# One core, a mixer and a three-pass MLP: VectorE's extra steps set one at a time at 13 spots of a group, and the first weight block of the second mixer half reloaded in parts

## What is computed

```python
def _rmsnorm(x, g): return x * rsqrt(mean(x * x) + EPS) * g
# mixer: u = hn @ w_in (1024 x 3072); an RG-LRU group and an HGRN2 group; y @ w_out
xp = xp + mixer(_rmsnorm(xp, ln_mix))
pn = _rmsnorm(xp, ln_mlp)
xp = xp + jnp.square(jax.nn.relu(pn @ w_up)) @ w_down       # D_FF = 4096
y = _rmsnorm(xp, ln_final)
```

## Time and profile before

| what | value |
|---|---|
| three runs | 2414.80, 2419.99, 2423.82 us |
| profiled execution | 2409.82 us, its span 2408.0 us |
| mean granted clock of TensorE | 0.974 |
| TensorE matmuls busy | 2253.4 us, 94% |
| VectorE busy | 1576.2 us, 65% |
| ScalarE busy | 1114.3 us, 46% |
| GpSimd busy | 1028.8 us, 43% |

### The profile page before, as it was taken

One profiled execution on the slowest core, in us unless ns is written; L12 is line 12 of the kernel. 1 busy time (PEld: TensorE's weight loads), 2 busy tenths in 40 slices (PEclk: granted clock), 3 DMA queues, 4 the chain that ended last, 5 costly groups with the idle time before them and its releaser, 6 DMA issues.

```text
span 2408.0 us, 43738 instructions
## 1 busy us (share of the span) xinstructions
PE 2253.4 (94%) x16512; PEld 2132.1 (89%) x16512; DVE 1576.2 (65%) x2884; ACT 1114.3 (46%) x2281; POOL 1028.8 (43%) x884
## 2 busy tenths in 40 slices
PE   9999999789999997999999978998889997899997
PEld 7878889778899987999999978998889997899997
DVE  8766663866666568766765286777676665765557
ACT  5444542445555554344344144554445454445554
POOL 2142102257777761000000035665556754566663
PEclk9999999899999998999999989999999999999998
DMA  9999955467765463322225334445556943354443
GB/s 347 274 300 293 260 159 209 129 182 207 205 175 168 144 188 94 105 88 89 83 76 189 110 108 158 136 135 168 159 168 181 315 119 95 107 158 151 133 129 115
DMA packets 239024, 397.78 MB, mean 165 GB/s; under 512 B 30944, under 2 KB 147808, under 8 KB 238816
## 3 DMA queue, kind: packets, MB, share of 16 engines
q1 hardware_dynamic: 187248, 262.71, 34.4%
q0 software_dynamic: 35872, 103.66, 16.6%
q10 hardware_dynamic: 15696, 28.61, 3.4%
HBM read 334.22 MB, written 127.77 MB: 192 GB/s over the span
## 4 chain that ended last, share of the span: by engine, by line
PE 72%; DVE 12%; ACT 6%; DMA 4%; issue 4%; POOL 2%; ACTq 1%; SPq 0%; DVEq 0%; POOLq 0%
PE bank L1068 10%; PE bank L1070 9%; PE bank L1069 9%; PE bank L1325 7%; PE bank L1327 6%; PE bank L1326 6%; PE aux L1325 6%; PE aux L1327 6%; PE aux L1326 6%; ACT w_hi L1416 2%; DVE dense L2593 2%; DMA w_st<-up_sums 2%; ACT dense L1416 2%; POOL w_lo L941 1%; PE aux L1265 1%
## 5 line engine op out<-in xcount | busy, mean ns | idle before, releaser
L941 POOL TENSOR_TENSOR w_lo<-w_st,w_hi 128x512 fp32r<-128x512 f32 x672 | 882.4, 1339 | 597.5 <-ACT w_hi L1416 596.3
L1416 ACT ACTIVATE w_hi<-w_st 128x512 fp32r<-128x512 f32 (+1 forms) x704 | 450.8, 649 | 518.9 <-PE aux L1327 273.7
L1068 PE MATMUL bank<-a_hi,w_hi 128*128 128x360 f32 (+4 forms) x1344 | 480.3, 357 | 14.6 <-DMA w_lo<-kept_lo 11.9
L1070 PE MATMUL bank<-a_hi,w_lo 128*128 128x360 f32 (+4 forms) x1344 | 462.8, 344 | 0.0
L1069 PE MATMUL bank<-a_lo,w_hi 128*128 128x360 f32 (+4 forms) x1344 | 462.3, 344 | 0.0
L1325 PE MATMUL bank<-dense,w_hi 128*128 128x328 f32 (+2 forms) x768 | 256.3, 334 | 36.1 <-DVE dense L2593 22.1
L1325 PE MATMUL aux<-dense,w_hi 128*128 128x328 f32 (+2 forms) x768 | 252.6, 329 | 37.5 <-DVE xy L2660 37.5
L1068 PEld LDWEIGHTS bank<-a_hi,w_hi 128*128 128x128 f32 x1344 | 253.9, 189 | 37.5 <-DVE xy L2660 8.1
L1069 PEld LDWEIGHTS bank<-a_lo,w_hi 128*128 128x128 f32 x1344 | 254.5, 189 | 16.8 <-issue 1.6
L1070 PEld LDWEIGHTS bank<-a_hi,w_lo 128*128 128x128 f32 x1344 | 253.9, 189 | 16.2
L1327 PE MATMUL aux<-dense,w_lo 128*128 128x328 f32 (+2 forms) x768 | 250.3, 326 | 0.0
(11 more groups left out here) (322 smaller groups left out, 4395.8 us busy)
## 6 DMA issues: line engine op xcount, KB each, us to landing
w_st<-up_sums SPq DMA_DIRECT2D x192, 256.0 KB, 2.7
w_st<-down_sums SPq DMA_DIRECT2D x384, 128.0 KB, 2.2
w_st<-in_wall SPq DMA_DIRECT2D x144, 256.0 KB, 2.7
w_st<-in_wall SPq DMA_DIRECT2D x288, 128.0 KB, 2.3
up_sums<-in_wall POOLq DMA_DIRECT2D x40, 512.0 KB, 13.8
down_sums<-in_wall POOLq DMA_DIRECT2D x40, 512.0 KB, 20.8
w_st<-in_wall SPq DMA_DIRECT2D x32, 512.0 KB, 8.0
kept_hi<-w_hi SPq DMA_DIRECT2D x32, 512.0 KB, 9.8
```

The lines of the kernel that those rows point to most:

```text
L941: pool.tensor_tensor(w_place(w_lo, h), w_place(w_st, h), w_place(w_hi, h).bitcast(F32), ALU.subtract).then_inc(w_ready, 1)
L1068: pe.matmul(ps, wh, xh, start=(j == 0), stop=False)
L1070: mm = pe.matmul(ps, wl, xh, start=False, stop=(j == 7))
L1416: return nc.scalar.activation(out, in_, func, **kw)
```

## The change

VectorE's extra steps get 13 numbered spots in a group, one step at each: spots 0 to 2 ahead of the up stage's first gather, 3 and 4 behind the first and second gather, and in the down stage spot 5 + 2j inside pair j, between take 6 and takes 2, 3 and 4, and spot 6 + 2j behind the pair. spare(q, g, n) says what stands at a spot. ScalarE's high parts and squares and SyncE's stores are placed to suit (SPOT_AT, SPOT_STORE). The operands ahead begin at spot 8 of group 2 and end at spot 4 of group 6. The sums of squares stand in groups 1 and 2 of pass 2, TensorE's sum and ScalarE's root in group 3, the two inverses in groups 4 and 5, the scaling in groups 5 and 6, and the stores of it in groups 6 and 7. Of to_basis only the first pair's two additions stay between the quarters; the others go to spots 5 to 10.

At the handover the first weight block is reloaded in two column halves, each as soon as its old content is used up and before both of GpSimd's adds, with semaphores of its own; the second add goes behind the reload of block 1. The loads of x are issued up to two halves later, and NF, FN and FY three slots later. basis_pair and unmix are cut into halves of one instruction each (basis_half, unmix_half; the waits stay).

The parts of the diff are in the order of the file: constants, SyncE, GpSimd, TensorE, ScalarE, VectorE.

```diff
-LATE = 1
+LATE = 2
-X_LOADS = {15: (0, 1), 16: (2,), 18: (3,), 19: (4,), 21: (5,), 22: (6,), 23: (7,)}
+X_LOADS = {15: (0,), 17: (1,), 18: (2,), 20: (3,), 21: (4,), 22: (5,), 23: (6, 7)}
...
-AHEAD_G = 3
 RIGHT_D[2] = [s_ for steps in AHEAD for s_ in steps]
-STORE_AT = [23, 26, 30, 33]
+SPOT_AT = {3: 0, 4: 1, 5: 14, 6: 15, 7: 17, 8: 19, 9: 21, 10: 22, 11: 24, 12: 26}
+SPOT_STORE = {3: 9, 4: 10, 5: 23, 6: 25, 7: 27, 8: 28, 9: 30, 10: 32, 11: 34, 12: 35}
+SPOTS = 13
+
+def _ahead_spots():
+    at, g, n = {}, 2, 8
+    for op in RIGHT_D[2]:
+        while n < 3 and op[0][0] == "l":
+            n += 1
+        at[g, n] = op
+        g, n = (g, n + 1) if n + 1 < SPOTS else (g + 1, 0)
+    return at
+
+AHEAD_AT = _ahead_spots()
+HIGH_AT = {(g, SPOT_AT[n]): ("hi" + op[0][2], op[1]) for (g, n), op in AHEAD_AT.items() if op[0][0] == "l"}
+STORE_AT = {HALVES * g + SPOT_STORE[n]: RIGHT_A.index(("hi" + op[0][2], op[1]))
+            for (g, n), op in AHEAD_AT.items() if op[0][0] == "l"}
+ADD_AT = {(1, n): n - 3 for n in range(3, 13)} | {(2, n): n + 7 for n in range(3, 9)}
+SQUARE_AT = {(g, SPOT_AT[n]): m for (g, n), m in ADD_AT.items()}
...
-FINAL_SLOTS = {9: ("NF", 0), 10: ("FN", 0), 11: ("FN", 1), **{13 + b: ("FY", b) for b in range(8)}}
+FINAL_SLOTS = {12: ("NF", 0), 13: ("FN", 0), 14: ("FN", 1), **{16 + b: ("FY", b) for b in range(8)}}
...
-                for n in range(len(AHEAD)):
-                    if h - STREAM == HALVES * (AHEAD_G + n // PAIRS) + STORE_AT[n % PAIRS]:
-                        keep_ahead(2 * n)
-                        keep_ahead(2 * n + 1)
+                if h - STREAM in STORE_AT:
+                    keep_ahead(STORE_AT[h - STREAM])
...
+            pool.wait_ge(w_kept[0], 32 * (MLP0 // 2))
+            for half in range(2):
+                c = slice(HW * half, HW * (half + 1))
+                pool.wait_ge(product_done, down_no(0, GROUPS - 1, PAIRS - 1, ORDER[2 * half]))
+                pool.dma_start(w_hi[:, 0, c], kept_hi[0][:, c]).then_inc(w_first[half], 16)
+                pool.dma_start(w_lo[:, 0, c], kept_lo[0][:, c]).then_inc(w_first[half], 16)
             add_input_square(1 + DVE_SQUARES)
-            pool.wait_ge(w_kept[0], 32 * (MLP0 // 2))
-            pool.wait_ge(product_done, down_no(0, GROUPS - 1, PAIRS - 1, ORDER[2]))
-            reload(0, 0)
-            add_input_square(2 + DVE_SQUARES)
             pool.wait_ge(w_kept[1], 32 * (MLP0 // 2))
             pool.wait_ge(product_done, down_no(0, GROUPS - 1, PAIRS - 1, ORDER[-1]))
             reload(1, 1)
+            add_input_square(2 + DVE_SQUARES)
...
-                if p and blk < MLP0:
-                    pe.wait_ge(w_again[blk % 2], 32 * (blk // 2 + 1))
+                if p and blk == 0:
+                    pe.wait_ge(w_first[0], 32)
+                elif p and blk < MLP0:
+                    pe.wait_ge(w_again[blk % 2], 32 * ((blk + 1) // 2))
...
+                    elif p and (blk, t) == (0, 0):
+                        pe.wait_ge(w_first[1], 32)
...
+                    if q == 1 and (g, at) in HIGH_AT:
+                        act.wait_ge(next_normed, 2 * KB)
+                        right_high(2, *HIGH_AT[g, at])
+                    if q == 2 and (g, at) in SQUARE_AT:
+                        final_square(1, SQUARE_AT[g, at] // 4, SQUARE_AT[g, at] % 4)
...
-                        if q == 1 and AHEAD_G <= g < AHEAD_G + 4 and at in (17, 20, 24, 27):
-                            n = PAIRS * (g - AHEAD_G) + (17, 20, 24, 27).index(at)
-                            if n < len(AHEAD):
-                                for name, kb in RIGHT_A[2 * n:2 * n + 2]:
-                                    right_high(2, name, kb)
-                        elif (q, g) == (2, LATE) and at in (18, 22, 25):
-                            final_squares(1, (at - 18) // 3)
...
-                        if part == 2 and g in (LATE + 2, LATE + 3):
-                            t = g - LATE - 2
+                        if part == 2 and g in (6, 7):
+                            t = g - 6
...
-                    if i == 7 and g:
+                    if i == 7 and g == 0:
+                        dve.wait_ge(basis, 2 * (PAIRS * q + j + 1))
+                    elif i == 7:
                         dve.wait_ge(product_read, take_no(q, g - 1, j, 4))
...
+                    spare(q, g, 5 + 2 * j)
...
-                def to_basis(q):
-                    if q == 1:
-                        dve.wait_ge(old_in[2], 16 * KB)
-                    if q < 2:
-                        for j in range(PAIRS):
-                            basis_pair(q, j)
-                    dve.wait_ge(basis, PAIRS * (q + 1))
+                def spare(q, g, n):
+                    if q < 2 and g == 0 and 5 <= n < 11:
+                        basis_half(q, (n - 3) // 2, (n - 5) % 2)
+                    if q == 1 and g in (1, 2):
+                        if g == 1 and n >= 5:
+                            next_norm(n - 5)
+                        elif g == 2 and n < 8:
+                            next_norm(8 + n)
+                    if q == 1 and (g, n) in AHEAD_AT:
+                        dve.wait_ge(next_normed, 2 * KB)
+                        right_step(2, *AHEAD_AT[g, n])
+                    if (q, g) == (1, GROUPS - 1) and n >= 5:
+                        basis_half(2, (n - 5) // 2, (n - 5) % 2)
+                    if q == 2 and g == 0 and n >= 5:
+                        unmix_half(1, (n - 5) // 2, (n - 5) % 2)
+                    if q == 2 and (g, n) in ADD_AT:
+                        add_final(1, ADD_AT[g, n])
+                    if q == 2 and g in (LATE + 2, LATE + 3) and n == 0:
+                        middle_inverse(g - LATE - 2)
+                    if q == 2 and g in (5, 6) and n >= 5:
+                        middle_out(KB * (g - 5) + n - 5)
...
-                    to_basis(q)
+                    if q < 2:
+                        for half in range(2):
+                            basis_half(q, 0, half)
...
+                    for n in range(3):
+                        spare(q, g, n)
                     for j in range(2):
-                        for i in (5, 7, 6):
+                        for n, i in enumerate((5, 7, 6)):
                             gather(q, g, j, i)
+                            if j == 0 and n < 2:
+                                spare(q, g, 3 + n)
                         quarters(q, g, j)
...
                         takes(q, g, j)
+                        spare(q, g, 6 + 2 * j)
-                        elif q == 1 and g in (1, 2):
-                            for n in range(2):
-                                next_norm(KB * (g - 1) + 2 * j + n)
-                        elif q == 1 and AHEAD_G <= g < AHEAD_G + 4:
-                            n = PAIRS * (g - AHEAD_G) + j
-                            if n < len(AHEAD):
-                                for name, kb in AHEAD[n]:
-                                    right_step(2, name, kb)
-                        elif (q, g) == (1, GROUPS - 1):
-                            basis_pair(2, j)
-                        elif (q, g) == (2, 0):
-                            unmix(1, j)
-                        elif (q, g) == (2, LATE):
-                            for i in range(4):
-                                add_final(1, 4 * j + i)
-                        elif (q, g) == (2, LATE + 1):
-                            for i in range(4):
-                                middle_out(4 * j + i)
```

More of the change, by code:

```diff
@@ L517, in build @@
         w_again = [sem("w_again0"), sem("w_again1")]
+        w_first = [sem("w_first0"), sem("w_first1")]
         unit_done = sem("unit_done")
@@ L2392, in weight_rest, with unmix_half, unmix @@
                    ALU.subtract).then_inc(w_ready, 1)
-            def unmix(q, j):
+            def unmix_half(q, j, half):
                 x11, x12, x21, x22 = quadrants(q, j)
                 dve.wait_ge(product_read, take_no(q, GROUPS - 1, j, 4))
-                tt(x12, x12, x22, ALU.subtract).then_inc(unmixed, 1)
-                tt(x21, x21, x22, ALU.add).then_inc(unmixed, 1)
+                if half == 0:
+                    tt(x12, x12, x22, ALU.subtract).then_inc(unmixed, 1)
+                else:
+                    tt(x21, x21, x22, ALU.add).then_inc(unmixed, 1)
+            def unmix(q, j):
+                for half in range(2):
+                    unmix_half(q, j, half)
             for p in range(2):
@@ L2690, in takes, with basis_half @@
                         unmix(q, j)
-                def basis_pair(q, j):
+                def basis_half(q, j, half):
                     x11, x12, x21, x22 = quadrants(q, j)
-                    tt(x12, x12, x22, ALU.add)
-                    tt(x21, x21, x22, ALU.subtract).then_inc(basis, 1)
-                def to_basis(q):
-                    if q == 1:
-                        dve.wait_ge(old_in[2], 16 * KB)
-                    if q < 2:
-                        for j in range(PAIRS):
```

(15 more changed lines are left out.)

9 lines of the change are left out of this document (1 added, 8 removed).

## The result

The changed kernel takes 2345.25 us (median of 4 runs, 2340.55 to 2349.92) against 2417.39 before (4 runs, 2413.68 to 2423.82): ratio 0.970, 95% interval 0.967 to 0.973. Run once more beside other kernels it gave 2344.31 and 0.970 (0.967 to 0.972). The forecast was 2350, its range 2334 to 2390. The profiled execution took 2349.92, the longest of the four; its span is 2348.1.

A forecast was written before the change was run, and what follows sets the result against it. TensorE, 94% busy, plus its waits for VectorE's late takes was taken as the bound. Terms 29.1 + 2.6 + 25.3 + 7.3 + 11.6 - 6.5 = 69.4 us gave 2340.4, with 10.2 from profile to median 2350, range 2334 to 2390.

The forecast's parts named there:

- Operands ahead: Second pass, groups making the third pass's operands: single steps remove take waits, 21.9 us, and lost clock, 7.2: 29.1 us.
- Squares, inverses, scaling: Third pass: blocks become single steps, removing 19.0 us of TensorE idle time and 6.3 of clock: 25.3 us.
- First groups: First and second pass: only two of eight to_basis steps stay between quarter chains, saving 3.5 and 3.8 us: 7.3.
- Group 7 of the second pass: Basis steps for the third pass change place there: bounds 0 and 5.3 us, half taken, 2.6.
- Handover: Change to the second mixer half: (a) gives 4.1 us, (b) and (c) together 7.5: 11.6 us.
- (a): Handover: spacing the loads of x makes ScalarE's square, VectorE's adds and the takes earlier: 4.1 us.
- (b): Handover: first weight block no longer waits 7.83 us; mostly covered by late a_lo tiles, so 2 us taken.
- (c): Handover: NF moves by three half units, 5.8 us, over a 5.19 us wait; with (b) 7.5 us.
- Cost of the spots: Thirteen groups with single steps in the down stage: 0.5 us each, bounds 0 and 3.0: 6.5 us lost.
- the first: Rival: each single step meets a GpSimd split, taking 1.78 us, 39 lost over thirteen groups: 2383; chance 0.15.
- The second rival: The handover gives nothing, as later loads of x delay adds and a_lo tiles: 58 us stay, 2362; chance 0.10.
- The fourth: Rival: the two-place ring of operand stores binds from a 4.7 us landing; at 6.7 us 104 lost, 2454; chance 0.04.

The follow-up runs named there:

- e12: The kernel before, unchanged, run once more with a second profile: 2420.12 us, ratio 1.002.
- e2: The kernel before with only the three handover edits (loads of x, slots of NF/FN/FY, reload of first weight block): 2409.98 us, ratio 0.996.
- e3: The changed kernel with all eight basis steps back between the quarter chains of group 0, first and second pass: 2350.89 us, ratio 0.973.
- e6: The changed kernel with GpSimd's weight splits cut to 128 of 512 columns from group 1 of the second pass, result not the reference's: 2336.05 us, ratio 0.967.
- e4: The changed kernel with the old slots for the loads of x alone: 2343.50 us, ratio 0.969.
- e9: The changed kernel itself, run once more with a second profile: 2344.31 us, ratio 0.970.
- e5: The changed kernel with the last two adds of the squares of x moved from GpSimd to VectorE: 2339.51 us, ratio 0.969.
- e7: The changed kernel with each operand tile made ahead stored to three places, ScalarE waiting for all three: 2378.28 us, ratio 0.985.
- e8: The changed kernel with old loads of x, last two square adds on VectorE, and VectorE's first square add one pair later: 2339.90 us, ratio 0.969.
- e10: e5 with old loads of x and GpSimd's two loads of each made operand issued one half unit apart: 2342.57 us, ratio 0.970.
- e11: e5 with old loads of x and ScalarE instead of GpSimd issuing the loads of made operands: 2341.16 us, ratio 0.969.

## Why the prediction was right

Its main step held: blocks of extra work made the takes late, the takes made TensorE pause, and behind most of the longer pauses the clock fell as well. That each late take costs twice, as the prediction has it, is too strong: its one row was such a case, and nine of fourteen were (e12). The term itself stood on the mean clock of the stretch and does not suffer by it. What no run separates is what of the spots' gain comes from single steps and what from their places: the spots also put five of the thirteen steps of a group into the up stage, and ScalarE's and SyncE's parts moved along. By its own terms:

- *Operands ahead*: 29.1 forecast. 31.4 and 35.0 by the two pairs of profiles. The first profile of before, on which the sum stood, had the same pauses as the second and less of the lower clock; in e2, without the spots, the four groups took 247.9 us.
- *Squares, inverses, scaling*: 25.3 forecast; groups 1 to 3 of the third pass lost 24.1 and 27.7.
- *First groups*: 7.3 forecast; e3 gives 5.6 to 6.6, the cost of six spots included.
- *Group 7 of the second pass*: 2.6 forecast, none came: 60.0 and 59.9 became 61.0 and 62.1 (59.7 in the mean of three profiles without the spots, 60.4 in that of the eight with them and the loads and splits as they were). The collision is what costs there (e6), and the new places met it just the same.
- *Handover*: 11.6 forecast, 9.1 in e2. Its step (a), that spaced loads of x would make the square and so the take earlier by 4.1 us, is wrong: e4 without it is no slower, and the product behind that take starts at 896.8 with it and without. Steps (b) and (c) were put at 7.5. All three together gave 9.1 us (e2), and undoing them costs 2356.5 - 2344.8 = 11.7; with (a) worth nothing, (b) and (c) were probably put too low, by less than these runs can tell for sure. They were not undone one by one. The a_lo wait that (b) foresaw came, as 3.21 + 2.73 us instead of the 7.83 for the weights; the gate's wait fell from 5.19 to 0.95.
- *Cost of the spots*: 6.5 forecast. Groups 1 and 2 of the second pass are 113.5 us in the mean of ten profiles with the spots, 111.0 in three without: 2.5 for two groups. With the short splits of e6 they are 109.5, so what they lose is the collision with the splits. In groups 3 to 6 all of TensorE's pauses are 0.6 us, in groups 1 and 2 of the third pass 0.06. That is 3.2 us without group 7, so the term was put about 3 us too high. The prediction took its windows a little off the groups: groups 1 and 2 of the second pass run from 1483.2 to 1594.3 in the kernel before, not from 1520 to 1606; all sixteen scalings lie inside its window even so.
- *From profile to median*: 10.2 us were added. e12 and e9 bear this out: it was chance in one profile.

The errors, 2 to 6 us each, had both signs and nearly cancelled: 75.9 - 6.5 = 69.4 forecast, 72.1 measured. Of the rivals, the first (each single step meets a split) is false as it was priced: outside group 7 single steps take 0.65 to 1.12 us on the mean, not 1.78, and the half of the low parts that were shortest took 0.53 or less. e6 shows that its mechanism is real: it is worth 0.3 us a group in groups 3 to 6, 2 us a group in groups 1 and 2, and some 6 in group 7. By the Trainium skill (SBUF — State Buffer, "SBUF: two separate sides"), the lock blocks a VectorE step for the GpSimd operation that it meets; e5 and e6 agree: with the adds off GpSimd the waits for a_lo fell from 5.9 to 1.3 us (e5), with short splits a low part from 0.65 to 0.53; in group 7 a step was held for a run of three splits, not for one. But by the rule alone the change would have gained half of what it did. A single step does not wait for a whole split each time: GpSimd is busy for 147.62 of 218 us, and most of the low parts passed beside it. In groups 1, 2 and 7 of the second pass the rule did speak against the change: there it gained nothing or lost a little. The second rival was right in half, its spaced loads gave nothing, and wrong on the reload. The third falls: VectorE's total never was the limit. The fourth did not come, with a landing of 3.7 us; e7 shows that its ring is real and its price too high.

## What to carry to other kernels

When an in-order engine with a third of its time free still makes the bound engine wait, look for its blocks: split them to one step at a place, each shorter than the slack there. Count what the clock loses behind the pauses too, but by the mean over a stretch: here nine of fourteen pauses of 2 to 3 us were followed by the lower clock, and not the same ones in each execution. Undo each part in a run by itself: here one of three edits at one place was worth nothing or less, and the total hid it. Once the large pauses are gone, removing one of 3 us moves it on (e5, e8, e10, e11); compare the sum of two neighbouring stages, not one.

## What the runs showed of the hardware

- A VectorE step with two inputs was held to the end of a run of three GpSimd splits, not of one split: 3.42 and 4.28 us beside runs of 3.78 and 3.79, and 0.53 to 0.60 in e6 when the splits are a quarter as wide. The second of these steps starts 0.1 us ahead of the run by the rows and was held all the same.
- A step that stands alone is not always shorter than one of two in a row: a low part went from 0.97 to 0.65 us, a scaling of next_norm from 0.99 to 1.12. With short splits they take 0.53 and 0.60, so what counts is which of them meets a split.
- A pause of TensorE of 2.1 to 3.2 us was followed by the lower clock in nine cases of fourteen, and not the same ones each time: the pause of 3.05 us in group 3 of one profile was not, the same pause in the other (3.06 us) was.
- One kernel's profiled span varied by 11 us (2408.0 and 2419.0) with the same instructions, the mean granted clock 0.974 and 0.968. In groups 3 to 6 the pauses differed by 0.8 us and the length by 4.5. A difference of 60 us between two profiles stood for 72 between medians.
